# Feed-forward entry of a decoder step: residual squares taken inside the output projection, token sums on VectorE, up-projection weights loaded earlier

## The reference

```python
merged = g_sb * o_sb.reshape(B, L, W_Q) + g_fx * o_fx.reshape(B, L, W_Q)
x = x + jnp.einsum('blm,md->bld', merged, w_o)             # output projection, 2048 x 2048
h = _rms_norm(x, g_ffn)                                    # y = x * rsqrt(mean(x*x) + eps) * g
u = jnp.square(jax.nn.relu(jnp.einsum('bld,df->blf', h, w_up)))   # up, 2048 x 8192
return x + jnp.einsum('blf,fd->bld', u, w_down)            # down, 8192 x 2048
```

## Time and profile before

| what | us |
|---|---|
| median of 3 runs | 3426.97 |
| range of the 3 | 3426.41 to 3435.69 |
| the profiled execution, its own time | 3426.94 |
| its span, first to last instruction | 3425.4 |

### The profile page before, as it was taken

One profiled execution on the slowest core, in us unless ns is written; L12 is line 12 of the kernel. 1 busy time (PEld: TensorE's weight loads), 2 busy tenths in 40 slices (PEclk: granted clock), 3 DMA queues, 4 the chain that ended last, 5 costly groups with the idle time before them and its releaser, 6 DMA issues.

```text
span 3425.4 us, 68044 instructions
## 1 busy us (share of the span) xinstructions
PE 3223.9 (94%) x25065; PEld 3058.6 (89%) x25065; DVE 1913.1 (56%) x2498; ACT 1405.5 (41%) x1860; POOL 376.0 (11%) x622
## 2 busy tenths in 40 slices
PE   5999999999999989997789759999999999999999
PEld 5999999999999988773369759999999999999998
DVE  4224656654554458878752277788877443333333
ACT  4223555554554446666631234444443222212211
POOL 0111111111111123223310030000000000000000
PEclk8999999999999999999999979999999999999999
DMA  4433333333343338779973325444444533333332
GB/s 145 124 106 108 96 102 103 95 99 94 106 112 93 99 84 292 252 252 348 330 251 88 97 66 138 129 123 135 135 129 123 192 111 123 111 119 115 113 96 86
DMA packets 498966, 472.63 MB, mean 138 GB/s; under 512 B 22817, under 2 KB 421026, under 8 KB 497330
## 3 DMA queue, kind: packets, MB, share of 16 engines
q1 hardware_dynamic: 458866, 354.34, 35.0%
q0 software_dynamic: 40032, 117.38, 10.3%
HBM read 426.85 MB, written 44.80 MB: 138 GB/s over the span
## 4 chain that ended last, share of the span: by engine, by line
PE 86%; DVE 4%; DMA 4%; issue 2%; ACT 1%; POOLq 1%; POOL 1%; SPq 0%; DVEq 0%; ACTq 0%
PE ps L764 26%; PE ps L765 25%; PE ps L766 25%; PE ps L961 3%; PE ps L969 2%; PE ps L970 2%; PE ps L894 1%; DVE pg_lo L1558 1%; POOLq L446 1%; DMA w_raw<-in_w_up_dram 1%; DMA pg<-in_cache_sb_v_dram 1%; PE ps L808 1%; DVE x2T L1976 0%; PE ps L818 0%; DMA w_raw<-in_cache_sb_v_dram 0%
## 5 line engine op out<-in xcount | busy, mean ns | idle before, releaser
L764 PE MATMUL ps<-h_hi,w_hi 128*128 128x260 f32 (+1 forms) x2592 | 756.2, 292 | 13.0 <-DVE h_lo L1558 10.1
L765 PE MATMUL ps<-h_hi,w_lo 128*128 128x260 f32 (+1 forms) x2592 | 736.2, 284 | 0.0
L766 PE MATMUL ps<-h_lo,w_hi 128*128 128x260 f32 (+1 forms) x2592 | 734.7, 283 | 0.0
L1558 DVE TENSOR_TENSOR w_lo<-w_raw,w_hi 128x2048 fp32r<-128x2048 f32 (+1 forms) x241 | 471.1, 1955 | 264.4 <-ACT w_hi L1166 229.6
L1166 ACT ACTIVATE w_hi<-w_raw 128x2048 fp32r<-128x2048 f32 x160 | 305.8, 1911 | 696.8 <-PE ps L766 693.0
L764 PE MATMUL ps<-ub_hi,w_hi 128*128 128x260 f32 x2048 | 580.6, 284 | 7.8 <-DVE ub_lo L1558 4.4
L766 PE MATMUL ps<-ub_lo,w_hi 128*128 128x260 f32 x2048 | 579.9, 283 | 0.0
L765 PE MATMUL ps<-ub_hi,w_lo 128*128 128x260 f32 x2048 | 579.7, 283 | 0.0
L764 PE MATMUL ps<-b_hi,w_hi 128*128 128x260 f32 x1792 | 508.9, 284 | 57.7 <-DVE b_lo L1558 45.2
L765 PE MATMUL ps<-b_hi,w_lo 128*128 128x260 f32 x1792 | 508.6, 284 | 0.0
L766 PE MATMUL ps<-b_lo,w_hi 128*128 128x260 f32 x1792 | 508.4, 284 | 0.0
(11 more groups left out here) (268 smaller groups left out, 5232.2 us busy)
## 6 DMA issues: line engine op xcount, KB each, us to landing
w_raw<-in_w_in_dram SPq DMA_DIRECT2D x81, 1024.0 KB, 5.9
w_raw<-in_w_down_dram SPq DMA_DIRECT2D x64, 1024.0 KB, 5.3
w_raw<-in_w_up_dram SPq DMA_DIRECT2D x32, 1024.0 KB, 9.4
u_raw<-in_w_up_dram SPq DMA_DIRECT2D x32, 1024.0 KB, 8.5
u_dram<-u_out SPq DMA_DIRECT2D x32, 520.0 KB, 2.9
u_st<-u_dram SPq DMA_DIRECT2D x8, 2080.0 KB, 7.8
w_raw<-in_w_out_dram SPq DMA_DIRECT2D x16, 1024.0 KB, 5.8
kraw<-kT_dram POOLq DMA_DIRECT2D x32, 264.0 KB, 3.1
```

The source lines that it names most:

```text
L764: pe.matmul(out, whi, xhi, start=first, stop=False, skip_group_check=more)
L765: pe.matmul(out, wlo, xhi, start=False, stop=False, skip_group_check=more)
L766: return pe.matmul(out, whi, xlo, start=False, stop=last, skip_group_check=more)
L1558: return dve.tensor_tensor(out, a, hi.bitcast(F32), ALU.subtract)
```

## The change

Five edits that belong together.

1. The squares of block n are taken by ScalarE inside the output projection, right after the split of the next slab, and VectorE adds them up in `n2_ss` (15 additions of 128x520). TensorE's 32 small matmuls of the norm become 2.
2. The spill of `x2T` is cut in two halves of 2.08 MB. The first goes after the load of the last slab; then come the first unit's two weight slabs, as soon as `w_raw` is free; the second half of the spill follows the last add. `first_sums` and `second_sum` of unit (0, 0) move ahead of the last slab's adds, `low` 5 and 1 ahead of `normed`.
3. The four token differences leave GpSimd and stand on VectorE (`token_sum`); `normed` works on whole 520-token blocks (16 instructions instead of 32); `TOKENS` becomes 1, 5, 2, 6, 7, 3, 4, and ScalarE's and VectorE's lists follow it.
4. The odd unit's weights and the unit outputs lie in blocks of `x2T` whose token operand is already split: the odd unit's first slab over tokens of product 1 (needs `b_lo_ok` 1), the second over those of product 3 (needs `b_lo_ok` 6). The odd unit's two loads become four of 512 KB, and each unit's one store becomes two.
5. Some waits on `a_sum_ok` go, `up_ld` counts each slab apart, and the final transposes reuse older semaphores.

```diff
@@ buffers @@
-        u_raw = [at(f"u_raw{k}", [P, KT, P], F32, at_r + 6240 + 8192 * k) for k in range(2)]
-        u_out = [at(f"u_out{k}", [P, 2, TQ], F32, at_r + 6240 + 16640 + 4160 * k) for k in range(2)]
+        u_odd = [x2T[:, 8 * i:8 * i + 8, HQ * i:HQ * i + 2 * P] for i in range(2)]
+        u_raws = [[[w_raw[i][:, 8 * k:8 * k + 8, :] for k in range(2)] for i in range(2)],
+                  [[u_odd[i][:, :, P * k:P * k + P] for k in range(2)] for i in range(2)]]
+        u_out = [x2T[:, 1:5, HQ:TQ].rearrange("p (m h) t -> p m h t", m=2),
+                 x2T[:, 8:12, 0:HQ].rearrange("p (m h) t -> p m h t", m=2)]
-        TOKENS = (1, 5, 6, 2, 7, 3, 4)
+        TOKENS = (1, 5, 2, 6, 7, 3, 4)
@@ SP @@
+            def up_slab(g, i):
+                src = wup_v[:, :, bass.ds(g[0] * (4 * P) + (g[1] * 2 + i) * P, P)]
+                if g[1] == 0:
+                    sp.dma_start(w_raw[i][:, :, :], src).then_inc(up_ld[0][i], 16)
+                else:
+                    for e in range(2):
+                        sp.dma_start(u_raws[1][i][e], src[:, 8 * e:8 * e + 8, :]).then_inc(up_ld[1][i], 16)
...
-                two = u_dram[bass.ds(g[0] * 4 + 2 * p, 2)].rearrange("m p t -> p m t")
                 sp.wait_ge(u_ok, count(g, 3, 3))
-                sp.dma_start(two, u_out[p][:, :, :]).then_inc(u_sv[p], 16)
+                for m in range(2):
+                    slab_of = u_dram[bass.ds(g[0] * 4 + (2 * p + m), 1)].rearrange("o p (h t) -> p (o h) t", h=2)
+                    sp.dma_start(slab_of, u_out[p][:, m, :, :]).then_inc(u_sv[p], 16)
...
-            sp.wait_ge(evac_v, 32 + FREE_DENSE)
-            sp.dma_start(x2_dram, x2T[:, :, :]).then_inc(x2_sv, 16)
-            sp.wait_ge(w_lo_ok, S_WO + KT)
-            up_load((0, 0))
-            sp.wait_ge(b_sum, 4)
-            sp.wait_ge(b_lo_ok, 7)
-            up_load((0, 1))
+            sp.wait_ge(evac_v, 16 + FREE_DENSE)
+            sp.dma_start(x2_dram[:, 0:8, :], x2T[:, 0:8, :]).then_inc(x2_sv, 16)
+            sp.wait_ge(w_lo_ok, S_WO + KT)
+            for i in range(2):
+                up_slab((0, 0), i)
+            sp.wait_ge(evac_v, 32 + FREE_DENSE)
+            sp.dma_start(x2_dram[:, 8:16, :], x2T[:, 8:16, :]).then_inc(x2_sw, 16)
+            sp.wait_ge(b_lo_ok, 1)
+            up_slab((0, 1), 0)
+            sp.wait_ge(b_lo_ok, 6)
+            up_slab((0, 1), 1)
@@ POOL @@
-            pool.tensor_tensor(b_t[:, :, :], part(0, 1), part(0, 0), ALU.subtract).then_inc(b_sum, 1)
...
-            pool.tensor_tensor(part(8, 0), part(8, 0), b_t[:, :, :], ALU.subtract).then_inc(b_sum, 1)
@@ TensorE @@
-            norm_pe(1, n2_sq, HQ)
+            pe.wait_ge(ss_ok, KT - 1)
+            for half in range(2):
+                mm = pe.matmul(ps[:, B_O + half, 0:HQ], ones[:, :], n2_ss[:, half * HQ:(half + 1) * HQ], start=True, stop=True)
+            mm.then_inc(nrm["ss"], 1)
@@ ScalarE @@
+            def square(j, u):
+                n = j * 2 + u
+                act.wait_ge(evac_v, j * 4 + (2 * u + 2 + FREE_DENSE))
+                wait(act, ss_ok, n - 2 if isinstance(n, int) else j * 2 + (u - 2))
+                dst = n2_ss if isinstance(n, int) and n == 0 else n2_sq[u]
+                act.activation(dst[:, :], x2T[:, bass.ds(n, 1), :].rearrange("p o t -> p (o t)"), ACT.Square).then_inc(nrm["sq"], 1)
...
             act.wait_ge(evac_v, 32 + FREE_DENSE)
-            norm_act(1, x2T, n2_sq, n2_rs, HQ)
...
-            for o in (5, 1, 6, 2):
-                high((0, 0), o)
-            for o in TOKENS[:4]:
+            high((0, 0), 5)
+            high((0, 0), 1)
+            norm_rs(n2_rs, HQ, KT + 1, 2)
+            for o in TOKENS[:2]:
+                token_high(o)
+            high((0, 0), 6)
+            high((0, 0), 2)
+            for o in TOKENS[2:4]:
                 token_high(o)
@@ VectorE @@
+            def square_sum(j, u):
+                dve.wait_ge(nrm["sq"], j * 2 + (u + 1 + KT))
+                wait(dve, ss_ok, j * 2 + (u - 1))
+                dve.tensor_tensor(n2_ss[:, :], n2_ss[:, :], n2_sq[u][:, :], ALU.add).then_inc(ss_ok, 1)
...
-            first_sums((0, 0))
-            second_sum((0, 0))
-            dve.wait_ge(nrm["rs2"], 2)
-            dve.wait_ge(x2_sv, 16)
...
+            wout(Slab(S_WO + 14), Slab(S_WO + 15), 14, (6, 1))
+            first_sums((0, 0))
+            second_sum((0, 0))
+            wout(Slab(S_WO + 15), None, 15, (7, 0))
+            square_sum(7, 1)
+            low((0, 0), 5)
+            low((0, 0), 1)
+            dve.wait_ge(nrm["rs2"], 2)
+            dve.wait_ge(x2_sv, 16)
+            normed(0)
+            dve.wait_ge(y_ok, 1)
+            token_sum(5)
+            token_low(1)
+            dve.wait_ge(x2_sw, 16)
+            normed(8)
+            dve.wait_ge(y_ok, 2)
+            token_sum(7)
+            token_low(5)
+            token_sum(6)
+            token_low(2)
+            low((0, 0), 6)
+            low((0, 0), 2)
+            token_low(6)
+            token_sum(4)
+            last_sum((0, 0))
```

More of the change, by code:

```diff
@@ L338, in build @@
         m_full, m_hi_ok, m_lo_ok, x_ld = (sem(n) for n in ("m_full", "m_hi_ok", "m_lo_ok", "x_ld"))
-        up_ld = [sem(f"up_ld{k}") for k in range(2)]
+        up_ld = [[sem(f"up_ld{k}_{i}") for i in range(2)] for k in range(2)]
         a_sum_ok, a_hi, a_lo = sem("a_sum_ok"), sem("a_hi"), sem("a_lo")
@@ L375, in source @@
         def source(o, p):
[L377 to L379 removed]
+            (a11, a12), (a21, a22) = u_raws[p]
+            return {1: a11, 2: a12, 4: a22, 5: a_sum[0][:, :, :], 6: a_sum[1][:, :, :], 7: a21, 3: a12}[o]
         def part(k0, half):
@@ L529, in _ @@
                     slab(Slab(S_WO + u, j * 2, j), wout_v[:, :, bass.ds(j * (2 * P) + u * P, P)])
[L531 to L538 removed]
+            def up_slab(g, i):
[5 more added lines that the diff above has]
+                        sp.dma_start(u_raws[1][i][e], src[:, 8 * e:8 * e + 8, :]).then_inc(up_ld[1][i], 16)
+            def up_load(g):
+                sp.wait_ge(a_lo, count(g, 7, -7))
+                for i in range(2):
+                    up_slab(g, i)
             def up_store(g):
                 p = g[1]
[L542 removed]
                 sp.wait_ge(u_ok, count(g, 3, 3))
[L544 removed]
+                for m in range(2):
+                    slab_of = u_dram[bass.ds(g[0] * 4 + (2 * p + m), 1)].rearrange("o p (h t) -> p (o h) t", h=2)
+                    sp.dma_start(slab_of, u_out[p][:, m, :, :]).then_inc(u_sv[p], 16)
             def stage(c, done=None):
@@ L1192, in _ @@
             split_hi(Slab(0))
-            norm_act(0, xT, n_sq, n_rs, HT)
+            for k in range(KT):
+                if k >= 2:
+                    act.wait_ge(nrm["ss"], k - 1)
+                act.activation(n_sq[k % 2][:, :], xT[:, k, :], ACT.Square).then_inc(nrm["sq"], 1)
+            norm_rs(n_rs, HT, KT, 1)
             for k in range(KT):
@@ L1439, in _ @@
                 act.activation(m_hi[:, 4 * k:4 * k + 4, :], mraw[:, 4 * k:4 * k + 4, :], ACT.Copy).then_inc(m_hi_ok, 1)
+            def square(j, u):
[4 more added lines that the diff above has]
+                act.activation(dst[:, :], x2T[:, bass.ds(n, 1), :].rearrange("p o t -> p (o t)"), ACT.Square).then_inc(nrm["sq"], 1)
             split_hi(Slab(S_WO + 1), Slab(S_WO))
-            with act.Fori(0, KT // 2 - 1) as j:
+            for i in range(4):
+                split_hi(Slab(S_WO + 2 + i), Slab(S_WO + 1 + i))
+                square(i // 2, i % 2)
+            with act.Fori(2, KT // 2 - 1) as j:
                 for u in range(2):
                     split_hi(Slab(S_WO + 2 + u, j * 2, j), Slab(S_WO + 1 + u, j * 2, j))
+                    square(j, u)
+            for u in range(2):
+                square(KT // 2 - 1, u)
             act.wait_ge(evac_v, 32 + FREE_DENSE)
-            norm_act(1, x2T, n2_sq, n2_rs, HQ)
             def high(g, o):
@@ L1978, in normed, with token_sum @@
                 ins.then_inc(y_ok, 1)
+            def token_sum(o):
+                out, x, y = {5: (b_t[:, :, :], part(0, 1), part(0, 0)), 7: (part(0, 1), part(8, 1), part(0, 1)),
+                             6: (b_t[:, :, :], part(8, 1), b_t[:, :, :]), 4: (part(8, 0), part(8, 0), b_t[:, :, :])}[o]
+                if o == 6:
+                    dve.wait_ge(b_lo_ok, 2)
+                if o == 4:
+                    dve.wait_ge(b_sum, 3)
+                dve.tensor_tensor(out, x, y, ALU.subtract).then_inc(b_sum, 1)
@@ L1988, in _ @@
+            token_sum(5)
             token_low(1)
-            normed(8, 1)
-            normed(8, 0)
+            dve.wait_ge(x2_sw, 16)
[5 more added lines that the diff above has]
+            token_low(2)
             low((0, 0), 6)
             low((0, 0), 2)
+            token_low(6)
+            token_sum(4)
             last_sum((0, 0))
-            for o in TOKENS[1:4]:
-                token_low(o)
```

137 lines of the change are left out of this document (52 added, 85 removed).

## The result

| | median us | lowest to highest | runs |
|---|---|---|---|
| before | 3430.06 | 3426.41 to 3435.69 | 4 |
| changed | 3390.65 | 3386.67 to 3392.89 | 4 |

The ratio is 0.9882, with a 95% interval of 0.9864 to 0.9901. The forecast was 3384.8 us (a ratio of 0.9877) with a range of 3379 to 3395. The measured time lies in the range, 5.9 us above the forecast.

The account below looks back on a forecast made before the run. It took the 102 us between output and up projection, where TensorE works 43 us, as the bound; product 3 starting 42.2 us earlier gave 3426.94 - 42.2 = 3384.7, forecast 3384.8 us, range 3379 to 3395.

Parts of the forecast that it names:

- What bounds the kernel: Between output and up projection, 102 us with TensorE working 43; the forecast is new starts for products 1 and 3.
- Up to product 1: Last add to first up product: weight wait leaves the path, small steps remain; start at 1949.9, 21.6 us earlier.
- Up to product 3: First unit: one unbroken VectorE queue, then the odd unit's second slab lands; product 3 at 1987.1, 42.2 us earlier.
- Both bounds of the text: Landing of the odd unit's second slab: 5.8 us like a lone 1 MB slab (taken), or 9.95 like a pair.
- Two fixed costs one after the other: Odd unit's second slab in two halves: if each paid the DMA fixed cost in turn, product 3 starts 2 us later.
- The differences on VectorE: First unit: four differences add 9.2 us to VectorE's queue, paid for because nobody waits for GpSimd any more.
- one pair of rows: GpSimd's last difference, 2003.45 to 2010.11, beside VectorE's 1.2 us weight split from 2005.52, which took 5.67.
- The clock: After each pause TensorE restarts at 1.2 GHz; the first product then takes 4.8 us instead of 2.9.
- Elsewhere: Steady units unchanged, extra loads and stores hidden; down projection staging may cost or save 1.5 us; fewer end waits: nothing.
- the slower rival: Odd unit's weights late in every pair: 15 units stall 6.3 us each, 3479; chance 0.02, plus 0.03 for a part.
- The sum: Whole kernel: 3426.94 - 42.2 = 3384.7 us for the profiled execution; forecast 3384.8.
- It is hardly waited for: Odd unit's second slab lands within 3.4 us, VectorE's queue sets product 3 at about 1984.6; gain 44.7, 3382; chance 0.08.

Follow-up runs that it names:

- each part undone: Four kernels, each the changed kernel with one part put back (squares, spill order, GpSimd differences, odd slabs), one run each: 3404.35, 3409.27, 3399.05 and 3398.81 us.
- the first profile: First profiled execution of the changed kernel, nothing further changed: 3390.59 us, 1452.0 us from last add to end, down projection 764.56 us.
- the two measurements: The changed kernel against the kernel before, measured twice with four runs each: medians 3390.65 and 3390.14 us, ratios 0.9882 and 0.9884.

## Why the prediction was right, point by point

**What bounds the kernel.** It named two starts, of product 1 and of product 3, and each part undone moved one or both of these. Beyond them the steady units were to stay, and did.

**Up to product 1.** Forecast 14.7 us after the last add, measured 14.66. The small steps came as worked out: the 128x520 addition 0.70 (0.7 was forecast), eight instructions of `normed` 5.46 (5.5), a difference 2.33 (2.33). The weight pair landed 10.3 us after its issue (10.4).

**Up to product 3.** Product 6: forecast +33.8, measured +33.72. Product 3: forecast +51.9, measured +52.29. The term that was off is the landing of the lone slab: 6.4 us after its issue at 1979.91, against the 5.8 taken; the issue itself came 0.3 us earlier than forecast, which leaves 0.4. Both bounds of the text stood, 5.8 and 9.95, and the value lay near the lower. Two fixed costs one after the other would have made it 2 us; 0.6 were found.

**The differences on VectorE.** They were to add 9.2 us to its queue and be paid for by nobody waiting for GpSimd. With them put back on GpSimd, product 3 is 10.5 us later. The exclusion that the prediction read from one pair of rows is part of this, GpSimd's own pace the rest. The prediction named one stretched instruction; the trace before has three, 13.1 us in sum.

**The clock.** The prediction had TensorE restart at the lower level after each pause. For the pauses of 4.7 to 25 us ahead of products 1, 6 and 3 this holds in both traces. Behind shorter ones it is not general: behind the 2.35 us at 2011.58 some seven matmuls ran 0.12 us apart, at full clock, and only then some fifteen 0.22 us apart, at the lower one, and behind third pauses of up to 2.12 us in the down projection the clock stayed at 1.00.

**Elsewhere.** The mechanism was right and one size was not. The steady units did not stall; the slower rival (loads into strided blocks landing after 15 us) is out: the halves of 512 KB landed in 5.9 us, the median from 2040 to 2600 us. The staging was allowed to cost or save 1.5 us and carried no value in the sum. This is the step that was mis-sized: the two stores cost some 0.7 us there on average, and in the first profile the later landing and the lower clock behind the longer pause brought the loss to 3.8 us. The sum set nothing for a place where a wait for stores stood ahead of the staging in SP's list, although the change doubled those stores, and it counted a pause without the clock behind it.

**The sum.** The stretch gained 41.85 us for 42.2 forecast. The changed kernel's median is 5.9 us above the forecast, and so is its profiled execution (3390.59). There the terms can be read off: 1.8 us ahead of the last add, where two executions of one kernel differ by more than that, 0.35 up to product 3, -0.2 up to the down projection and 3.8 inside it. For the medians the base counts as well: the forecast was made against 3426.94, while four executions of the kernel before have a median of 3430.06 and seven later ones 3429.68. As a ratio the forecast was 0.9877, the two measurements 0.9882 and 0.9884; that these agree to 0.0007 is partly luck, since the interval is 0.9864 to 0.9901.

**Rivals.** *It is hardly waited for* gave +49.4 for product 3 if the slab came in time; the run that sends it earlier has +49.12, so this rival was a correct reading of what is late next, not of the change as it stands.

## What to carry to other kernels

Where a phase boundary idles the main engine, list every chain that ends there, and move them together: here early squares with late weights bought nothing and early weights with late squares 8.9 of 21.6 us, because one hid under the other. Send the next phase's first weights as soon as their buffer is free and put bulk spills around them, not ahead of them. When an edit adds stores to a queue, look for the one place where the queue stands still until they have landed, and move that wait to where the data is really needed. Before a longer pause is put down to what was changed, look at when it began and not only at its length.
